# First block rebuilt: split fp32r tiles on the raw input, norms applied at eviction, attention by head pairs with a projection tile in each step

## The reference

```python
h = rmsnorm(x, attn_norm_g)                       # (512, 1024)
gla_q, gla_k, gla_v, gla_r, gla_lr, mb_q, mb_k, mb_v, mem_q = split(h @ w_in)
g_log = log_sigmoid(gla_lr @ w_gla_gk + b) / 16   # 4 heads, dk 64, dv 128, chunks of 64
o_gla = rmsnorm(gla_chunked(gla_q, gla_k, gla_v, g_log)) * silu(gla_r)
q_b, k_b = rmsnorm(mb_q), rmsnorm(mb_k)           # 4 heads of 64
o_moba = moba_attention(q_b, k_b, mb_v, slopes)   # causal, ALiBi; with 512 tokens all past blocks are chosen
mem_k, mem_v = split(rmsnorm(mem) @ w_mem_kv)     # 256 memory tokens
o_mem = memory_attention(rmsnorm(mem_q), rmsnorm(mem_k), mem_v)
x = x + concat(o_gla, o_moba, o_mem) @ w_out
x = x + hierarchical_moe(rmsnorm(x), ...)         # top-1 group, top-2 of its 8 experts, 32 experts
```

## Time and profile before

| | |
|---|---|
| time, median of 3 runs | 1987.58 us (1985.32 to 1987.82) |
| time of the profiled execution | 1985.14 us |
| its span | 1983.1 us |
| busy: PE, DVE, ACT, POOL | 1807.2, 720.2, 557.6, 492.9 us |
| first gather of the experts begins at | 467.84 us |

### The profile page before, as it was taken

The page is one execution under the profiler, slowest core; times in us unless marked ns, Lnnn a source line. Parts: engine busy times, 40 slices in busy tenths (PEclk is TensorE's granted clock), DMA queues, the critical chain, the costliest instruction groups (busy, mean ns, idle before and its releaser), DMA issues.

```text
span 1983.1 us, 19881 instructions
## 1 busy us (share of the span) xinstructions
PE 1807.2 (91%) x8122; PEld 1215.5 (61%) x8122; DVE 720.2 (36%) x1083; ACT 557.6 (28%) x739; POOL 492.9 (25%) x211
## 2 busy tenths in 40 slices
PE   6767996886999999999787999999999999999995
PEld 4534554354444444443466889777777788888883
DVE  4323344334333333334696111223335431212235
ACT  2232232112100110101454214555433342323231
POOL 1000000003101111100223443544444344434340
PEclk9888997977999999999998999999999999999998
DMA  7111111502999999999312211021223232232201
GB/s 266 40 40 43 43 43 42 215 0 81 421 421 421 421 421 420 421 421 412 102 43 85 85 65 64 3 83 43 85 85 128 85 127 85 85 127 85 85 32 43
DMA packets 79595, 308.52 MB, mean 156 GB/s; under 512 B 3584, under 2 KB 4880, under 8 KB 54800
## 3 DMA queue, kind: packets, MB, share of 16 engines
q1 hardware_dynamic: 79232, 306.16, 39.4%
q0 software_dynamic: 272, 1.05, 0.2%
HBM read 305.10 MB, written 2.10 MB: 155 GB/s over the span
## 4 chain that ended last, share of the span: by engine, by line
PE 83%; DVE 9%; ACT 3%; issue 2%; POOL 1%; DMA 1%; SPq 0%; DVEq 0%; ACTq 0%
PE ps L815 36%; PE ps L1103 11%; PE ps L877 8%; PE ps L1127 6%; PE ps L1057 3%; PE ps L872 3%; PE ps L813 2%; PE ps L1250 2%; PE ps L1072 1%; PE ps L958 1%; PE ps L1073 1%; ACT sb_slot L1317 1%; PE ps L1235 1%; PE ps L1271 1%; DVE sb_R L2122 1%
## 5 line engine op out<-in xcount | busy, mean ns | idle before, releaser
L748 POOL TENSOR_TENSOR sb_w_parts<-sb_slot,sb_w_parts 128x2048 fp32r<-128x2048 f32 x59 | 274.5, 4653 | 412.3 <-ACT sb_w_parts L1317 412.3
L815 PE MATMUL ps<-sb_h_high,sb_w_parts 128*128 128x512 f32 x1120 | 275.2, 398 | 15.2 <-issue 8.2
L815 PEld LDWEIGHTS ps<-sb_h_high,sb_w_parts 128*128 128x128 f32 x1120 | 212.5, 191 | 67.2 <-issue 12.5
L1103 PE MATMUL ps<-sb_slot,sb_hT 128*64 128x512 f32 x768 | 171.1, 594 | 0.0
L815 PE MATMUL ps<-sb_hidden_high,sb_w_parts 128*128 128x512 f32 x704 | 165.2, 389 | 1.8 <-ACT sb_hidden_high L1317 1.8
L1317 ACT ACTIVATE sb_w_parts<-sb_slot 128x2048 fp32r<-128x2048 f32 x59 | 112.7, 1912 | 172.4 <-PE ps L815 172.4
L815 PEld LDWEIGHTS ps<-sb_hidden_high,sb_w_parts 128*128 128x128 f32 x704 | 132.1, 188 | 29.6 <-ACT sb_hidden_high L1317 2.3
L815 PE MATMUL ps<-sb_h_low,sb_w_parts 128*128 128x512 f32 x560 | 138.0, 389 | 0.0
L815 PEld LDWEIGHTS ps<-sb_h_low,sb_w_parts 128*128 128x128 f32 x560 | 105.3, 188 | 22.0
L1103 PEld LDWEIGHTS ps<-sb_slot,sb_hT 128*64 128x64 f32 x768 | 53.6, 137 | 106.2 <-issue 106.2
L877 PE MATMUL ps<-sb_hT,sb_slot 128*128 128x512 f32 x224 | 101.3, 607 | 0.0
(11 more groups left out here) (273 smaller groups left out, 2679.2 us busy)
## 6 DMA issues: line engine op xcount, KB each, us to landing
sb_slot<-w_gate SPq DMA_DIRECT2D x24, 2048.0 KB, 14.6
sb_slot<-w_up SPq DMA_DIRECT2D x24, 2048.0 KB, 15.1
sb_slot<-w_down SPq DMA_DIRECT2D x21, 2048.0 KB, 15.2
sb_slot<-w_in SPq DMA_DIRECT2D x19, 2048.0 KB, 7.9
sb_R<-w_down SPq DMA_DIRECT2D x11, 2048.0 KB, 15.6
sb_R<-w_gate SPq DMA_DIRECT2D x8, 2048.0 KB, 14.5
sb_R<-w_up SPq DMA_DIRECT2D x8, 2048.0 KB, 15.2
sb_slot<-w_mlp_up SPq DMA_DIRECT2D x8, 2048.0 KB, 8.5
```

The source lines that it names most:

```text
L748: nc.gpsimd.tensor_tensor(low, raw_part(g), high.bitcast(F32), ALU.subtract).then_inc(w_low, 1)
L815: ins = nc.tensor.matmul(o, w[:, k, at:at + P], h[:, k, :], start=first, stop=last)
L1103: ins = nc.tensor.matmul(ps_[b * CAP:(b + 1) * CAP, bank0, :], xgT[:, k, at:at + CAP], w[:, b, kk * 512:(kk + 1) * 512], start=(k == 0), s ...
```

## The change

The part up to the experts is rewritten. `TILES1` lists 32 projection tiles in the order of their use; the host lays each out as one 512 KB block, except the 16 columns of the gate's rank, which are a small load of their own. ACT rounds a tile's weights (`w1`), POOL makes the low part, and PE does 24 matmuls for a tile (`tile`, line 879). The moving operand is x times gain, split into high and low; the reciprocal root of the norm is multiplied in when DVE evicts the tile (line 1857). The same is done for the memory tokens. Value tiles are made feature-major too and transposed by PE (`turn_v`, 968). Queries aren't normalised: the sum over their head goes to rows (`rowsum`, 962) and is applied as a scale in the softmax; the gains of query and key are multiplied into the key.

The attention goes by 16 pairs, the MoBA pairs first. Step i does the scores of both heads on half the rows of the array (978), the turn of pair i-1 (986), the values of pair i-2 into half the columns each (999), one projection tile (two narrow ones in two steps), what belongs to the tile before, and from step 4 on a piece of the linear attention. At the end the output tiles 0 and 1 take the attention's half of their sum first. `norm 1` needs only four one-column sums (927), since router and turned tokens are made from x times gain and scaled afterwards; the router has its weights stationary, and the rank matmuls (1085) are bf16.

```diff
+    def tile(name, n):
+
+        g = TILES1.index((name, n))
+        if g + 1 < len(TILES1):
+            step("w1", g + 1)
+        job("tile", name, n)
...
+    fills = [[("mq", 1)], [("mv", 1)], [("ck", 0), ("cv", 0)], [("ck", 1), ("cv", 1)], [("cq", 0)], [("gk", 0)], [("gq", 0)],
+             [("cq", 1)], [("gv", 0)], [("gv", 1)], [("gk", 1)], [("gq", 1)], [("gv", 2)], [("gv", 3)], [("r", 0)], [("r", 1)]]
+    early = {0: ["mem_parts"], 1: ["mem_acc"], 4: [("decay", 0)], 5: [("decay", 1)], 10: ["lam"]}
+    late = {7: [("decay_qk", 0)], 8: [("turn_keys", 0), ("intra", 0)], 12: [("gla_out", 0), ("decay_qk", 1)], 13: [("gla_sum", 0)],
+            14: [("turn_keys", 1), ("intra", 1)], 15: [("gla_out", 1)]}
...
+    for i in range(len(PAIRS) + 2):
+        if i < len(PAIRS):
+            for hh in range(2):
+                jobs.append(("score", i, hh))
+            step("score", i)
+        if 1 <= i <= len(PAIRS):
+            for hh in range(2):
+                job("turn", i - 1, hh)
+        if i >= 2:
+            job("values", i - 2)
+        for e in middle.get(i, ()):
+            gla(*e)
+        if i < len(PAIRS):
+            step("soft", i)
+        if i >= 2:
+            step("low", i - 2)
+        for e in early.get(i, ()):
+            step(*((e,) if type(e) is str else e))
+        if i < len(PAIRS):
+            step("norm_rows", i)
+            for f in fills[i]:
+                tile(*f)
+            for f in fills[i]:
+                step("evict", *f)
+            if i == 1:
+                step("mem_sum")
+            if i == 0:
+                post("mk", 1)
+            else:
+                for f in fills[i - 1]:
+                    post(*f)
+            for e in late.get(i, ()):
+                gla(*e)
+        elif i == len(PAIRS):
+            gla("gla_sum", 1)
+            step("silu", 0, 2)
+            tile("r", 2)
+            step("evict", "r", 2)
+            step("mix", 0)
+            step("mix", 1)
+    tile("r", 3)
+    step("silu", 2, 3)
+    step("mix", 2)
+    step("evict", "r", 3)
+    step("silu", 3, 4)
+    step("mix", 3)
     for n in range(KD):
...
+TILES1 = [("mk", 0), ("mq", 0), ("mv", 0), ("mk", 1), ("mq", 1), ("mv", 1), ("ck", 0), ("cv", 0), ("ck", 1), ("cv", 1),
+          ("cq", 0), ("gk", 0), ("gq", 0), ("cq", 1), ("gv", 0), ("gv", 1), ("gk", 1), ("gq", 1), ("gv", 2), ("gv", 3)]
+TILES1 += [("r", n) for n in range(4)] + [("out", n) for n in range(KD)]
+KEYS, QUERIES, VALUES = ("mk", "ck"), ("mq", "cq"), ("mv", "cv", "gv")
+NORMED = [("mk", 0), ("mq", 0), ("mk", 1), ("mq", 1), ("ck", 0), ("ck", 1), ("cq", 0), ("cq", 1)]
+TURNED = [("mv", 0), ("mv", 1), ("cv", 0), ("cv", 1)] + [("gv", n) for n in range(4)]
+PAIRS = [(which, pr, qt) for which in ("moba", "mem") for pr in range(2) for qt in range(TT)]
...
+            for g in range(SLOTS1, 28):
+                tile_load(g)
+            taken(sp, ("values", len(PAIRS) - 1))
+            load(w_router, a["w_router"], ld["router"])
             chunk_load(2)
+            tile_load(28)
+            finished(sp, ("tile", "r", 3))
             chunk_load(3)
-            sp.wait_ge(o_done, 4)
-            load(w_router, a["w_router"], ld["router"])
+            tile_load(29)
+            sp.wait_ge(mix_gla, 4)
             chunk_load(4)
             chunk_load(5)
-            finished(sp, last_use("out0"))
+            tile_load(30)
+            tile_load(31)
             chunk_load(6)
+            sp.wait_ge(w1_low, len(TILES1))
+            chunk_load(1)
+            finished(sp, ("tile", "out", KD - 1))
+            chunk_load(0)
...
+                    pool.wait_ge(w1_high, g + 1)
+                    nc.gpsimd.tensor_tensor(w1_parts[g % 2][1], raw1[g % SLOTS1], w1_parts[g % 2][0].bitcast(F32),
+                                            ALU.subtract).then_inc(w1_low, 1)
...
+                for w_part, h_part in ((0, 0), (1, 0), (0, 1)):
+                    pe.wait_ge((w1_high, w1_low)[w_part], g + 1)
+                    for k in ks:
+                        if g == 0:
+                            pe.wait_ge((x_high, x_low)[h_part], k + 1)
+                        if (name, n) == ("ck", 0):
+                            pe.wait_ge((mem_up, mem_down)[h_part], k + 1)
+                        ins = nc.tensor.matmul(o[:, 0:width], w[w_part][:, k, :], h[h_part][:, k, :],
+                                               start=first and (w_part, h_part) == (0, 0) and k == ks[0],
+                                               stop=last and h_part == 1 and k == ks[-1])
...
+            def out_tile(n):
+
+                if n == 0:
+                    taken(pe, ("values", len(PAIRS) - 1))
+                    for m in range(2):
+                        tile("out", m, (4, 5, 6, 7), True, False)
+                    pe.wait_ge(mix_gla, 4)
+                    for m in range(2):
+                        tile("out", m, (0, 1, 2, 3), False, True)
+                elif n > 1:
+                    tile("out", n, range(KD), True, True)
...
+                        end(nc.tensor.matmul(o[hh][:, 0:w_], q_[half_of(hh), pr, qt * P:(qt + 1) * P], k_[half_of(hh), pr, 0:w_],
+                                             start=True, stop=True))
...
+                            v_ = (cvm if which == "mem" else vm)[:, pr, kt, half_of(hh)]
+                            ins = nc.tensor.matmul(o[half_of(hh), 0:P], v_, pT[i % 2][:, hh, kt, :], start=(kt == 0), stop=(kt == nk - 1),
+                                                   skip_group_check=True)
...
+                        v.scalar_tensor_tensor(out=HL[:, k, :], in0=xT[:, k, :], scalar=G("attn_norm_g", k), in1=HH[:, k, :].bitcast(F32),
+                                               op0=ALU.mult, op1=ALU.subtract).then_inc(x_low, 1)
...
+            def gla_norm(pr, hh):
+
+                taken(dve, ("gla_sum", pr, hh))
+                link(v.reciprocal(osq[:, hh, :], osq[:, hh, :]))
+                link(v.scalar_tensor_tensor(out=ogn[pr][:, hh, :], in0=ogn[pr][:, hh, :], scalar=G("gla_out_norm_g"), in1=osq[:, hh, :],
+                                            op0=ALU.mult, op1=ALU.mult))
...
+                    frees(v.tensor_tensor(dst, bank(job)[:, 0:w_], mem_rstd if name in ("ck", "cv") else rstd0, ALU.mult), job)
...
+                        fn(hT[:, n, :], xT[:, n, :], ACT.Copy, scale=G("ffn_norm_g", n)).then_inc(xg_ready, 1)
...
+                    fn(htok_high[:, t, cols], bank(st), ACT.Copy, scale=row_rstd[:, t:t + 1])
+                    frees(fn(htok[:, t, cols], bank(st), ACT.Copy, scale=row_rstd[:, t:t + 1]), st)
```

More of the change, by code:

```diff
@@ L989, in _ @@
[L989 to L1008 removed]
+                    for hh in range(2):
+                        taken(pe, ("turn_v", "gv", 2 * pr + hh))
@@ L2186, in constants @@
     put("eps", EPS)
+    put("eps64", EPS * CH)
     put("one", 1)
```

1073 lines of the change are left out of this document (560 added, 513 removed).

## The result

The changed kernel takes 1876.74 us in the median of 4 runs (1871.9 to 1883.12), the kernel before 1987.7 us (1985.32 to 1988.45, 4 runs in the same comparison): a ratio of 0.9447 (0.9415 to 0.9479). It is faster by 111 us; forecast were 159 us and 1828 us, and the range ended at 1872. The profiled execution took 1881.36 us, 4.6 us above the median.

A forecast was written before the change was run, and what follows sets the result against it. PE was taken to bound the experts and second block, left unchanged; before them it also waits. PE work 224 + waits 52 = 276 us, plus 33 puts the gather at 309, 159 us earlier: 1828 us, range 1796 to 1872.

The forecast's parts named there:

- the tail: From the last output tile to the first gather: 33 us, where it was 51.4 before.
- PE's work: All PE work up to the end of the last output tile, at the full clock: 224 us.
- Scores and values: Attention pairs on half rows or columns, taken to run side by side and so halved: 16.2 us.
- a rule's 19 us: Each change of array mode drains the engine: 80 changes at 0.236 us, 19 us, time 1847; nothing put in.
- Low clock: Low PE clock behind the three longest of the waits up to the last output tile: 8 us.
- Waits: PE's waits up to the last output tile: 44 us, or 52 us with the 8 us of low clock.
- `decay`: Steps 4 and 5: it stands on ACT and DVE between the exponentials and the row scaling, 3 us.
- the mix rounds: PE waits 4.5 us before the first half of output tiles 0 and 1 ends, for DVE's norm, evictions and four rounds.
- Steps bound by the chain: Rival: score, softmax, turn bound the steps, 11 us each in place of 7.5; 56 us more, 1884 us; chance 0.20.
- The weaker form: Rival: a DVE operation per step waits for POOL's whole 2.38 us, 32 us more, 1860 us; within the forecast's 0.66.
- halves don't overlap: Rival: no overlap of array halves at 128 columns, 16.2 + 5.7 us more, 1850 us; within the forecast's 0.66.
- The low clock: Rival: PE stays at 1.2 GHz over most of the new part; all of it gives 2052 us; chance 0.02.

The follow-up runs named there:

- e10: e9 with the high and low part of a weight tile side by side (stride 256) instead of one behind the other; 1849.5 us, ratio 0.9316.
- e6: e3 without the 28 matmuls of 64 columns that add carried states to linear attention's outputs (output lacks these terms); 1846.85 us, ratio 0.9292.
- e3: The changed kernel with both moves, `decay` and `lam` behind their step's row scaling and `chunk_state` behind the tile; 1865.34 us, ratio 0.9384.
- e2: The changed kernel with `chunk_state` (steps 11 and 15) behind the projection tile instead of ahead of it; 1869.14 us, ratio 0.9405.
- e7: e3 with ACT's rounding of the next weight tile ahead of the exponentials, and ahead of the mix rounds for output tiles 0 and 1; 1851.99 us.
- e4: The changed kernel with ten matmuls a tile instead of 24, most low-part products left out, read by its first gather (323.2 us); 1839.6 us.
- e5: e3 with scores and values reading all 128 rows or columns for each head instead of half (another output); 1868.68 us, ratio 0.9404.
- e1: The changed kernel with `decay` (steps 4 and 5) and `lam` (step 10) behind the softmax's row scaling; 1873.77 us, ratio 0.9433.
- e9: e7 with `decay` and `lam` behind their step's eviction, the memory tokens' sum in step 0, and the first two heads' norm over two steps; 1851.58 us.

## Why the prediction missed

The mechanism was right: one block in front of the experts, PE bound in most steps, experts and second block untouched, the tail at 31.7 us for 33. Three terms of the sum were too small, and together they are 58 us.

- **PE's work, 247 us for 224.** The tiles: 28 at 5.44 us were put in. Without a gap they take 5.60 (306.12 to 311.72 in the changed kernel), with what changes around them 5.71 (192.39 to 198.10), so 0.27 x 28 = 7.6 us more. Why 5.60 and not 5.44 stays open (e10), but the 5.71 stood in the trace of before, for tiles beside small matmuls, and the prediction took its price from tiles that stand alone. Scores and values: I halved them and read from the earlier trace rows that a change of mode is free. It costs 0.1 to 0.2 us, four times a step. A memory step takes 0.63 + 0.59 us for score and values and 0.16 more for the turn, 1.38 us where the sum had 0.43 + 0.47 = 0.90; over 16 steps that is 8 us. The prediction had named this cost as a rule's 19 us and set it to nothing. Outputs of linear attention, on PE's timeline of the changed kernel at the full clock:

```profile
198.77 0.49 PE L1045 MATMUL ps<-sb_R 128*128 128x128 f32 x2
199.19 0.66 PE L1050 MATMUL ps<-sb_slot,sb_R 64*128 64x64 f32 x4
199.77 0.49 PE L1045 MATMUL ps<-sb_R 128*128 128x128 f32 x2
```

  One tile of 128 tokens of one head (a product of 128 columns and two of 64, each in two records) takes 1.00 us, and 0.67 the first one, which has one state less (198.10 to 198.77). Four heads take 12 x 1.00 + 4 x 0.67 = 14.7 us, where 9.4 were put in: 5 us more. The three are 21 of the 23 us.
- **Low clock, 33 us for 8.** I charged it behind the three longest waits. It also falls behind waits of 2.5 to 6 us (step 11 above) and, what I had not considered, in gapless stretches of small matmuls, which this change makes. e6 shows this for the first pair. The linear-attention stage has 0.76 for a granted clock, and 21 of the 33 us. The two moves together gave back 9.4 us (e3) and leaving out the 64-column matmuls 4.8 (e6); the other 19 us no run here takes apart.
- **Waits, 54 us for 44.** `decay` was put at 3 us and was 10.6. ACT's three functions with a table load and POOL in DVE's way both counted. The banks behind `chunk_state`, 11.4 us, were not in the sum at all: I had followed the queues and not the rotation of seven banks. On the other side the start took 8.6 and not 11 us. e2 measures the banks at 7.6 us in the median, and e7 the order of the roundings at 13 (7.7 by the gather, most of it the clock), of which I had 1 for output tile 2 and a part of 4.5 for the mix rounds.

The rivals. Steps bound by the chain (1884): not as a rule, since in the stage from 126 to 160 us PE is busy for 34.00 of 34.00 us; but the time lies in this rival's part of the range, and e4 shows that the margin, for which I had 2.7 us (6.7 us of PE work against a chain of 4), is 1.2 us a step in the mean. The weaker form, a DVE operation held for POOL's whole duration, was the right mechanism where it struck (2.65 us above), and rare as forecast. That halves don't overlap is wrong as put: the overlap is there, and changes of mode take about half of it back. e5 puts what the halves save at 8.4 us of PE work, where I had 16.2, and at 3 us of time. The low clock was a rival of 0.02 for an all-or-nothing case, while a part of it, which is what came (33 us), stood in the sum with 8 us.

**What to carry on.** Small matmuls must be priced in their neighbourhood: a few records between changes of array mode cost more than the same records in a long group, and long runs of them can cost the clock for what follows. When PSUM banks go round in job order, write down for each job which earlier job holds its bank and when that is read; two more jobs in a step are enough to make a tile wait for the softmax of its own step. And a move of work in one queue pays only if what it is put in front of has slack: e1 and e9 mostly moved the waits, e2 removed one, and e7, which took a short operation whose input was long there ahead of one that had to wait, removed 11 us of waits and got some 9 back elsewhere, but lost less to the clock.

## What the runs showed of the hardware

- The granted clock was 0.54 in a stretch with PE busy for 15.00 of 15.00 us, in runs of 64- and 128-column fp32 matmuls (0.52 over 10.00 us in e3). It was 1.00 in the same place where the 64-column ones were left out (e6), but at the second such job it fell even so (0.57 over 4 us, behind waits of 0.3 to 0.6 us).
- A change between whole array, half rows and half columns cost 0.1 to 0.2 us beside groups of 4 to 8 records; four quarters do run side by side: e3's chunk states, 16 products of 128 columns in 32 records, take 1.10 us, where one after the other at 0.236 us each they would take 3.8.
- DVE's subtraction of two SBUF tiles took 2.65 us beside POOL, and the same one 0.69 us in e7, where POOL stood still.
